# Second block, first layer's attention: the scores of units 5, 10 and 16 one k-step later in TensorE's program

## The reference, cut to what matters

```python
def one_block(qs):
    qb1, qb2 = qs
    p1 = softmax(einsum('bqhd,bkhd->bhqk', qb1, k1) * scale)
    p2 = softmax(einsum('bqhd,bkhd->bhqk', qb2, k2) * scale)
    w = (p1 - lam * p2)
    return einsum('bhqk,bkhd->bqhd', w, v)
...
y_b = diff_attention(q1, q2, k1, k2, v, lam, lam_init, subln_g)
```

## Time and profile before

| what | value |
|---|---|
| median of 3 runs | 2048.92 us (2048.08 to 2048.97) |
| the profiled execution's own time | 2048.2 us |
| its span, first to last instruction | 2046.4 us |
| PE busy | 2002.6 us, 98% of the span |
| DVE busy | 1272.2 us, 62% |
| ACT busy | 795.7 us, 39% |
| mean granted clock of TensorE | 0.998 |

### The profile page before, as it was taken

How to read it: one execution, slowest core, us unless ns; L and a number is a source line. 1 busy time by engine, 2 the same in 40 slices (tenths; PEclk the granted TensorE clock), 3 DMA queues, 4 the chain that set the end, 5 groups by cost and what they waited for, 6 DMA issues and landing times.

```text
span 2046.4 us, 26524 instructions
## 1 busy us (share of the span) xinstructions
PE 2002.6 (98%) x11160; PEld 1776.3 (87%) x11160; DVE 1272.2 (62%) x1684; ACT 795.7 (39%) x1102; POOL 72.4 (4%) x81
## 2 busy tenths in 40 slices
PE   7999999999999999999999999999999999999998
PEld 5989888778888987899999999999887788888887
DVE  8476765876756996737546455464699745344443
ACT  4433334495253366534113122132537634232231
POOL 0000000000030000030000000001100010000001
PEclk9999999999999999999999999999999999999999
DMA  9543533634432531223323233232353222322221
GB/s 328 202 162 124 198 111 117 207 108 157 178 129 93 173 104 73 73 70 124 113 108 124 93 115 111 103 124 93 134 166 100 85 102 83 103 91 95 103 100 65
DMA packets 57702, 252.85 MB, mean 124 GB/s; under 512 B 6544, under 2 KB 14880, under 8 KB 39408
## 3 DMA queue, kind: packets, MB, share of 16 engines
q1 hardware_dynamic: 55552, 246.47, 35.1%
q0 software_dynamic: 592, 2.46, 0.4%
q10 hardware_dynamic: 1440, 2.24, 0.3%
HBM read 232.00 MB, written 12.06 MB: 119 GB/s over the span
## 4 chain that ended last, share of the span: by engine, by line
PE 55%; DVE 4%; issue 1%; ACT 1%; DVEq 0%; ACTq 0%
PE banks L2218 51%; DVE small L1555 1%; DVE prob L1578 0%; DVE aconv L1419 0%; PE banks L686 0%; PE banks L685 0%; PE banks L684 0%; DVE small L1558 0%; PE banks L752 0%; PE banks L738 0%; DVE dconv L1539 0%; DVE hxl L2650 0%; DVE ntx L2645 0%; PE banks L727 0%; PE banks L2146 0%
## 5 line engine op out<-in xcount | busy, mean ns | idle before, releaser
L2218 PE MATMUL banks<-hxh,whi_f 128*128 128x512 f32 (+1 forms) x1016 | 400.3, 394 | 6.7 <-ACT hxh L2419 2.8
L2601 DVE TENSOR_TENSOR wlo_f<-raw_f,whi_f 128x2048 fp32r<-128x2048 f32 x128 | 293.6, 2294 | 171.9 <-ACT whi_f L2379 171.8
L2218 PE MATMUL banks<-hxh,wlo_f 128*128 128x512 f32 (+1 forms) x1016 | 392.3, 386 | 0.0
L2218 PE MATMUL banks<-hxl,whi_f 128*128 128x512 f32 (+1 forms) x1016 | 380.8, 385 | 0.2 <-DVE hxl L2680 0.2
L2379 ACT ACTIVATE whi_f<-raw_f 128x2048 fp32r<-128x2048 f32 x130 | 248.2, 1909 | 294.4 <-PE banks L2218 276.3
L2218 PEld LDWEIGHTS banks<-hxh,whi_f 128*128 128x128 f32 x1016 | 191.8, 189 | 54.2 <-issue 16.1
L2218 PE MATMUL banks<-both_h,whi_f 128*128 128x384 f32 (+2 forms) x864 | 234.7, 342 | 3.1 <-ACT both_h L2419 1.0
L2218 PE MATMUL banks<-both_h,wlo_f 128*128 128x384 f32 (+2 forms) x864 | 230.7, 337 | 0.0
L2218 PE MATMUL banks<-both_l,whi_f 128*128 128x384 f32 (+2 forms) x864 | 228.1, 337 | 0.0
L2218 PEld LDWEIGHTS banks<-hxh,wlo_f 128*128 128x128 f32 x1016 | 191.7, 189 | 39.0
L2218 PEld LDWEIGHTS banks<-hxl,whi_f 128*128 128x128 f32 x1016 | 190.9, 189 | 35.5 <-DVE hxl L2680 0.8
(11 more groups left out here) (388 smaller groups left out, 3278.7 us busy)
## 6 DMA issues: line engine op xcount, KB each, us to landing
raw_f<-in_wst SPq DMA_DIRECT2D x133, 1024.0 KB, 4.9
mvr<-in_mst SPq DMA_DIRECT2D x120, 512.0 KB, 5.8
stack<-qk_parts SPq DMA_DIRECT2D x36, 192.0 KB, 6.7
x_kept<-xT SPq DMA_DIRECT2D x2, 2048.0 KB, 8.7
raw_f<-in_wst SPq DMA_DIRECT2D x8, 384.0 KB, 5.9
xT<-x_kept SPq DMA_DIRECT2D x2, 1536.0 KB, 8.9
qk_parts<-qk_h SPq DMA_DIRECT2D x3, 768.0 KB, 3.8
qk_parts<-qk_l SPq DMA_DIRECT2D x3, 768.0 KB, 3.9
```

The lines of the kernel that those rows point to most:

```text
L2218: last = pe.matmul(o, (wh, wl)[w][:, k, c, :], r[part][:, k, :], start=(k == order[0] and parts is not LOW and (w, part) == (0, 0)), stop= ...
L2601: dve.tensor_tensor(wlo[r][:], raw[r][:], whi[n % 2 if n > N_FIRST else n][:].bitcast(F32), ALU.subtract).then_inc(w_lo, 1)
```

## The change

One line of `Plan` changes. For layer 0 the table `early` gets entries of -1 for units 5, 10 and 16, so that `scores(v)` of these is one larger.

```diff
@@ class Plan, __init__
         self.a, self.b = (6, 68) if l == 0 else (6, 66)
-        self.early = {0: 1} if l == 0 else {0: 2, self.cut: 2}
+        self.early = {0: 1, 5: -1, 10: -1, 16: -1} if l == 0 else {0: 2, self.cut: 2}
```

## The result

The changed kernel takes 2053.56 us (median of 11 runs, 2051.61 to 2054.72), the kernel before 2048.92 (median of 11, 2046.26 to 2051.16). The ratio is 1.0022, with an interval of 1.0014 to 1.0029 at 95%: slower by 4.6 us in the medians, where 4.5 were forecast (2053.4). The profiled execution of the change took 2052.19 us, its span is 2050.4, 4.0 over that of before.

The account below looks back on a forecast made before the run. TensorE (PE), busy 98% of the span, was taken as the bound. Unit 5's 2.06, unit 10's 2.34 and unit 16's 0.1 sum to 4.5 us over the median 2048.92, forecasting 2053.4, range 2051.6 to 2054.3.

Parts of the forecast that it names:

- Unit 5: Scores 2.61 us later behind the values delay maxima, exponential and ACT's copy; PE stands 2.06 us before transpose L766.
- the two costs that had no row: Dearer scores behind the 24 small matmuls, and PE's restart after standing 2 us; 0 to 0.1 each, at two places.
- the lower end of the allowance: Of 4.5 to 4.9 us for the whole loss, 4.5 was taken.
- Unit 10: Same chain plus a 0.35 wait for L1075; maxima 3.05 later, PE stands 2.34 us before L766.
- Unit 16: PE's 0.53 wait moves to unit 17; 0.1 us lost, between 0.15 lost and 0.53 gained.
- its sign: Unit 16: the 0.53 wait before its scores gone, that before the scores of unit 17 grown to 0.9.
- The sum: Units 5, 10 and 16 together: 2.06 + 2.34 + 0.1 = 4.5 us slower.
- the hold at L766: PE's transpose waits for ACT's copy o_pair, queued behind the late first exponential; 2.06 us at unit 5, 2.34 at unit 10.
- That later waits give some back: Rival: two L706 waits behind the stalls vanish, 1.6 of 4.5 us, giving 2051.8; chance 0.16.
- That the copy is not held: Rival: copy L1122 not held behind the first exponential; no loss, at best 1.2 us gained, 2047.7; chance 0.08.
- That nothing happens: Rival: another wait comes first, so scores at units 5 and 10 start as today; 2048.9, chance 0.04.
- The clock behind a stall: Rival: clock falls behind the new stalls, 1.7 us per fall; 2055.1 with one, 2056.8 with two; chance 0.06.

Follow-up runs that it names:

- copy_first: Changed kernel, but ACT does the copy o_pair ahead of the first exponential of units 5 and 10; 2052.78 us, ratio 1.0028.
- u5_only: Kernel before with only the scores of unit 5 moved one k-step later; single run 2052.2 us, stretches 30.75 and 27.80.
- ahead_of_values: Changed kernel, but at units 5 and 10 the moved scores go ahead of the values in the shared k-step; 2050.04 us, ratio 1.0012.
- earlier: Kernel before with the scores of units 5 and 10 one k-step earlier, not later; single run 2053.37 us.
- tap_later: Kernel before with DVE doing no convolution tap in the two units where it splits a weight chunk; 2046.11 us, ratio 0.9990.
- both_edits: Kernel before with the convolution's taps later and transpose L766 of units 15 and 16 one k-step later; 2045.64 us, ratio 0.9986.
- joined16_later: Kernel before with transpose L766 of units 15 and 16 one k-step later; 2047.80 us, ratio 0.9999.

## Why the prediction was right

**Unit 5: 2.06 forecast, 2.22 measured, the same chain.** With 0.69 added the scores start at 728.58, as forecast to the hundredth, the maxima at 729.59 (forecast 729.48), the first exponential at 731.38 (731.28), the copy at 732.27 (732.17), L766 at 732.59 (732.50). The 0.1 is the first of the two costs that had no row: behind the 24 small matmuls the scores take 0.81 us (727.89 to 728.70) where they took 0.70, and DVE starts 1.01 behind their start, not 0.90. The second, the restart after the stall, is 0.07: the k-step comes 0.09 behind L766 where the trace of before has it 0.02 behind. I had taken the lower end of the allowance, "since the dearer pair is only exchanged for the one that the k-step pays now", and this reason fails. The exchange is there on PE: the first pair behind the scores takes 0.51 where the one behind the values took 0.62, and by the steps of 0.35 PE would be at L766 at 730.43 (0.69 added), as before at 730.44. But the chain that ends last runs from the scores through DVE and ACT, and it has the dearer scores without the cheaper k-step.

**Unit 10: 2.34 forecast, 2.63 measured.** Less 1.53, the context's steps start at 754.36 (754.32), the values at 755.27 (755.12), the scores at 756.73 (756.58), L766 at 760.75 (760.50). The new wait for L1075 was 0.34, forecast 0.35. The term was undersized by the same two costs, 0.1 behind the values and 0.06 for the restart at L766, and by 0.1 more for the step behind the wait for L1075, whose first matmul takes 0.23 to the next where it took 0.12.

**Unit 16: 0.1 forecast, 0.00 measured.** The scores come 0.36 later, not up to 0.62, because the k-step takes less than the 1.15 that I took as its most, and DVE is not free earlier. The wait before unit 17 grew to 1.13, where I had 0.9 as its sign.

**The sum** was 4.5, the stretches say 4.85, the ratio 4.5 (2.9 to 5.9) and the medians 4.6. That the whole agrees to 0.1 us while its terms are 0.35 too small together is luck: the medians themselves are known to no better than 1.5 us.

**What the term said too simply.** I wrote the hold at L766 as the cost of the late scores. It is what ends last, but copy_first shows that taking it away gives back 0.5 of 2.2 (and 0.6 of 2.6): the late exponentials stand behind it as the next limit, for which the scores of unit 6 then wait. The sum was not touched by this, since two limits side by side cost as much as the later one, but advice drawn from it (do the copy first) would have been nearly worthless.

**The rivals.** That later waits give some back: unit 5 alone gave 27.80 behind it, nothing back; the wait before unit 8 is 0.75 in the change and was 0.77; and the maxima of unit 6, by which I had said that it decides, are 2.22 later. That the copy is not held: excluded by the 2.00 and 1.99 at L766. That nothing happens: excluded by the stretches. The clock behind a stall: in 10 us around either new stall the granted clock is 1.00, that is 2.4 GHz, so it did not come in this execution, nor behind the stall of 2.00 in u5_only; behind longer ones it came (last section) (columns as in the earlier trace rows):

```profile
725.00:735.00 10.00, 8.00 (x64) 6.70 (x63) 5.92 (x8) 5.45 (x10) 0.00 (x0) 1.00 0.79 196
755.00:765.00 10.00, 7.67 (x60) 6.16 (x59) 6.24 (x10) 4.64 (x12) 0.00 (x0) 1.00 0.91 253
```

## What to carry to other kernels

Read a moved instruction against everything that shares its new slot: here the step was called one k-step late, but two thirds of the loss came with the 24 matmuls that the order within the slot put ahead of it, and a further third of a microsecond from a wait that the moved scores had covered. A late producer costs where an in-order engine has an unrelated copy queued behind it and another engine needs that copy; before mending that, ask what ends next, since the second limit may be only half a microsecond behind. And a wait of the busiest engine inside a loop is mended where the loop is paced (here by a tap of the convolution on DVE, one unit ahead), not by filling the wait.

## What the runs showed of the hardware that I had not expected

The granted clock fell in some executions of the same instructions and not in others, and mostly not behind a stall. Up to 2030 us the ten profiled executions show eleven falls from 2.4 to 1.2 GHz, each over some 3 to 7 us. Nine of them came within 2 us behind groups of matmuls of one column. Six lie near 598 us, behind sixteen such matmuls (L2119 and L2123); this is the fall of the earlier trace rows, and it is there in the kernel before and in ahead_of_values, copy_first, earlier, tap_later and both_edits. In the change and in the three others the same instructions ran at 2.4 GHz. The first of the sixteen and a later small matmul, in the kernel before:

```profile
595.83 1.05 PE L2119 MATMUL banks<-consts,nsq 128*128 128x1 f32 x8 [0.32 <-POOL nsq L2006]
...
598.33 0.42 PE L2218 MATMUL banks<-first_cl,whi_f 128*128 128x256 f32 x1
```

and in the change:

```profile
596.72 1.05 PE L2119 MATMUL banks<-consts,nsq 128*128 128x1 f32 x8 [0.31 <-POOL nsq L2006]
...
599.08 0.28 PE L2218 MATMUL banks<-first_cl,whi_f 128*128 128x256 f32 x1
```

From L2119 to the scores of unit 4 it is 124.8 us in the six executions with this fall and 123.2 in the four without, so the fall costs 1.6 us, where the prediction had 1.7. That is the head start of the change: it comes to L2119 0.89 later than before and to unit 4 0.68 earlier (719.97 against 720.65). Such falls are a part of the 3 to 5 us by which the whole times of one kernel spread.

Two falls lie near 1450 us (joined16_later and both_edits), behind L2119 and L2123 again, and PE did not wait ahead of these. The last of the nine was in joined16_later, where the clock was 0.69 in this stretch, in which PE never stood for more than 0.2 us:

```profile
795.00:805.00 10.00, 9.80 (x51) 8.78 (x50) 5.34 (x6) 6.48 (x20) 0.00 (x0) 0.69 0.00 0
```

What PE does there are the sums L791, eight matmuls of one column at a time, between k-steps:

```profile
796.62 0.60 PE L2218 MATMUL banks<-both_h,whi_f 128*128 128x512 f32 x2
...
797.77 0.95 PE L791 MATMUL banks<-consts,sqm 128*128 128x1 f32 x8
...
799.13 0.84 PE L2218 MATMUL banks<-both_l,whi_f 128*128 128x512 f32 x2
```

The pair of the last row takes 0.84 at 1.2 GHz, where the same pair takes 0.53 one k-step earlier (797.06), and the stretch from unit 14 to 15 became 1.34 us longer by it (38.54 against 37.20). These narrow matmuls are in every one of the kernels; the clock fell behind them here in this one of the ten executions. That they are what lets the clock fall is not shown, since no run leaves them out.

Two falls came behind a stall. In the run with the earlier scores the clock was 0.83 in the 10 us from 755, where PE waits 2.16 for L1075: the 24 small matmuls of the values there took 2.74 where they take 1.46, and by the share at half clock about 1.7 of the 4.8 us of that stretch are the clock's.

```profile
755.00:765.00 10.00, 7.84 (x53) 6.49 (x52) 5.01 (x7) 3.65 (x9) 0.00 (x0) 0.83 0.88 236
```

In u5_only PE stood longer than elsewhere near the start of the program, where in the kernel before it waits 0.95, and the clock was 0.83 in the 10 us from 50:

```profile
53.04 0.47 PE L2218 MATMUL banks<-hxh,whi_f 128*128 128x512 f32 x1 [2.66 <-ACT hxh L2419]
```

It comes to L2119 3.53 later than the kernel before, has no fall there, and so is 1.95 late at unit 4. The stalls of 2.00 and 1.99 in the change, and that of 2.00 in u5_only at L766, were nearly as long as 2.16 and cost no clock. The Trainium skill, page TensorE: Matmul & The Clock Gate, section What's actually happening, ties the clock to how busy PE has been of late. The runs agree with that for the two falls behind a wait; for the one at 798 us PE counts as busy for 98% of the stretch, so by the busy time of the profile the trace does not show it. Why these falls come in some executions and not in others was not tried.
